# Starting the first projection on the latent tokens alone, with the first weight chunk loaded in two halves

## The reference, cut to what matters

```python
silu_c, silu_cc = jax.nn.silu(c), jax.nn.silu(c_ctx)
# layer 0
shift, scale, gate       = jnp.split(silu_c  @ w_ada[0] + b_ada[0], 3, axis=-1)
shift_c, scale_c, gate_c = jnp.split(silu_cc @ w_ada[0] + b_ada[0], 3, axis=-1)
u  = x   * (1.0 + scale)   + shift        # 256 x 1024, the latents
uc = ctx * (1.0 + scale_c) + shift_c      # 256 x 1024, the other tokens
p  = u @ a_w_in[0]                        # 1024 x 2560: q, k, v and a gate
pc = uc @ a_w_in[0]
```

## Time and profile before

| what | us |
|---|---|
| median of three executions | 1200.04 (1199.06 to 1200.21) |
| the profiled execution | 1197.66 |
| its span, first to last instruction | 1195.8 |
| TensorE busy, of the span | 1145.7 (96%) |
| VectorE busy, of the span | 540.7 (45%) |
| DMA, mean over the span | 261 GB/s |

### The profile page before, as it was taken

How to read it: one execution, slowest core, us unless ns; L and a number is a source line. 1 busy time by engine, 2 the same in 40 slices (tenths; PEclk the granted TensorE clock), 3 DMA queues, 4 the chain that set the end, 5 groups by cost and what they waited for, 6 DMA issues and landing times.

```text
span 1195.8 us, 17528 instructions
## 1 busy us (share of the span) xinstructions
PE 1145.7 (96%) x7148; PEld 735.3 (61%) x7148; DVE 540.7 (45%) x1236; ACT 297.2 (25%) x722; POOL 22.8 (2%) x33
## 2 busy tenths in 40 slices
PE   4999999989999999999999899999999999999997
PEld 3486876668878888668886684444444444444442
DVE  3353439987566430792699722222222222222223
ACT  0000128860240001570521622211111111111112
POOL 0000000000000001120000000000000000000000
PEclk9999999999999999999999998999999999999999
DMA  9852219014343225467375987999999999999991
GB/s 339 330 211 71 71 70 353 2 39 171 119 166 119 93 71 167 112 181 235 141 287 192 349 205 313 427 428 427 428 429 429 427 429 426 430 429 429 429 420 64
DMA packets 82334, 312.59 MB, mean 261 GB/s; under 512 B 18129, under 2 KB 19228, under 8 KB 69338
## 3 DMA queue, kind: packets, MB, share of 16 engines
q1 hardware_dynamic: 78528, 309.03, 66.8%
q10 hardware_dynamic: 3530, 2.44, 0.7%
q0 software_dynamic: 208, 0.17, 0.1%
HBM read 310.45 MB, written 1.18 MB: 261 GB/s over the span
## 4 chain that ended last, share of the span: by engine, by line
PE 83%; DVE 12%; DMA 2%; ACT 2%; issue 1%; SPq 1%; DVEq 0%; ACTq 0%
PE ps L1270 18%; PE ps L903 17%; PE ps L1303 9%; PE ps L1236 5%; PE ps L1006 5%; PE ps L1248 5%; DVE G L2180 4%; PE ps L968 2%; PE ps L941 2%; PE ps L852 2%; PE ps L1111 2%; PE ps L1087 2%; PE ps L954 2%; PE ps L755 2%; DMA ring<-in_a_w_in 2%; DVE soft L1859 1%
## 5 line engine op out<-in xcount | busy, mean ns | idle before, releaser
L1270 PE MATMUL ps<-ring,prob 128*64 128x512 f32 x704 | 188.1, 592 | 0.0
L1270 PEld LDWEIGHTS ps<-ring,prob 128*64 128x64 f32 x704 | 60.9, 137 | 100.0 <-issue 99.9
L2335 DVE TENSOR_TENSOR prob<-ps,prob 128x512 f32<-128x512 f32 x16 | 17.2, 1076 | 191.9 <-PE ps L1270 191.9
L1303 PE MATMUL ps<-ring,prob 128*64 128x512 f32 x352 | 78.0, 595 | 0.0
L903 PE MATMUL ps<-U,ring 128*128 128x256 f32 x304 | 69.9, 380 | 1.6 <-DVE Q L2025 1.3
L1270 PE MATMUL ps<-K,prob 128*64 128x512 f32 x160 | 70.3, 592 | 0.0
L1236 PEld LDWEIGHTS ps<-bias,U 128*128 128x128 f32 x512 | 60.0, 196 | 13.7 <-issue 13.7
L1414 ACT ACTIVATE prob<-ps,soft 128x512 f32<-128x512 f32 (+2 forms) x112 | 65.0, 591 | 10.5 <-DVE soft L1864 8.5
L2343 DVE TENSOR_TENSOR probT<-ps,cst 128x512 f32<-128x512 f32 x32 | 22.1, 692 | 94.6 <-PE ps L1303 94.6
L903 PEld LDWEIGHTS ps<-U,ring 128*128 128x128 f32 x304 | 57.4, 190 | 10.1 <-DVE Q L2025 1.7
L1236 PE MATMUL ps<-bias,U 128*128 128x128 f32 x512 | 63.1, 283 | 0.0
(11 more groups left out here) (377 smaller groups left out, 1824.8 us busy)
## 6 DMA issues: line engine op xcount, KB each, us to landing
ring<-in_w_exp_gate SPq DMA_DIRECT2D x22, 2048.0 KB, 18.1
ring<-in_w_exp_up SPq DMA_DIRECT2D x20, 2048.0 KB, 16.5
ring<-in_w_exp_down SPq DMA_DIRECT2D x20, 2048.0 KB, 19.2
ring<-in_w_ada SPq DMA_DIRECT2D x12, 2048.0 KB, 16.4
ring<-in_w_mod SPq DMA_DIRECT2D x12, 2048.0 KB, 10.3
ring<-in_b_w_in SPq DMA_DIRECT2D x8, 2048.0 KB, 9.0
ring<-in_a_w_in SPq DMA_DIRECT2D x5, 2048.0 KB, 17.6
ring<-in_w_in SPq DMA_DIRECT2D x5, 2048.0 KB, 10.4
```

Of the source, the lines that this page charges most:

```text
L1270: last = mm(ps[x * CAP:(x + 1) * CAP, 2 + i, :], xg[:, k, x * CAP:(x + 1) * CAP], chunk(n, 2 * i + x, turn)[0][:, k, :], start=(k == 0), s ...
L1303: last = mm(ps[x * CAP:(x + 1) * CAP, 5 + c, :], hidT[:, k, x * CAP:(x + 1) * CAP], chunk(n, 4 + x, turn)[0][:, k, c * 512:(c + 1) * 512], ...
```

## The change

SP issues chunk 1 ahead of the latents' rows. Chunk 2, the first `a_w_in` chunk, is loaded in two DMAs of 1024 KB: its lower four row tiles in its old place in the order, with a semaphore of their own (`lower_in`), its upper four behind chunk 4. The context rows go behind the lower half.

TensorE streams chunks 0 and 1 first, then turns the latents' first four feature tiles, does both folds, turns the other four (two tiles to a bank) and the taps. Each lower job is now two jobs of 256 tokens: four matmuls on the latents, and later four on the context, into the two halves of the same bank. The turns of the context rows stand between the latents' jobs. The upper jobs are as before, over all 512 tokens, behind all lower ones. VectorE's copies of rows and its modulation follow that order: the first four latent tiles one by one, all further ones two at a time (128 x 512), and latents and context modulated apart in the lower features. The load of `a_sink` shares the semaphore of the taps.

The diff, cut to its core:

```diff
                 w = IN[src][l, :, c * COLS:(c + 1) * COLS].rearrange("(k p) n -> p k n", p=P)
-                sp.dma_start(slot(n), w).then_inc(full[n % SLOTS], 16)
-                if n in (0, 1):
-                    rows = IN[("x", "ctx")[n]][0].rearrange("(t p) f -> p t f", p=P)
-                    sp.dma_start(xrows[:, 2 * n:2 * n + 2, :], rows).then_inc(x_in[n], 16)
+                if n == PLACE["a_in"][0]:
+                    first_w = w
+                    sp.dma_start(slot(n)[:, 0:4, :], w[:, 0:4, :]).then_inc(lower_in, 16)
+                else:
+                    sp.dma_start(slot(n), w).then_inc(full[n % SLOTS], 16)
+                if n in (1, 2):
+                    rows = IN[("x", "ctx")[n - 1]][0].rearrange("(t p) f -> p t f", p=P)
+                    sp.dma_start(xrows[:, 2 * n - 2:2 * n, :], rows).then_inc(x_in[n - 1], 16)
+                if n == 4:
+                    first = PLACE["a_in"][0]
+                    sp.dma_start(slot(first)[:, 4:KT, :], first_w[:, 4:KT, :]).then_inc(full[first % SLOTS], 16)
...
             def turn_taps():
-                pe.wait_ge(taps_in, 16)
-                pe.wait_ge(vec_ok, 1)
+                pe.wait_ge(taps_in, 32)
+                pe.wait_ge(x_ok, 4)
...
-            def turn_rows(half):
-                pe.wait_ge(x_in[half], 16)
-                for j in range(KT):
-                    i = half * KT + j
-                    if i >= 4:
-                        pe.wait_ge(x_ok, i - 3)
+            def turn_rows(half, js, bank):
+                for i, j in enumerate(js):
                     for t in range(2):
-                        last = tr(ps[:, 1 + j % 4, t * P:(t + 1) * P], xrows[:, 2 * half + t, j * P:(j + 1) * P], ident)
-                    last.then_inc(pe_x, 1)
+                        last = tr(ps[:, bank, i * S + t * P:i * S + (t + 1) * P],
+                                  xrows[:, 2 * half + t, j * P:(j + 1) * P], ident)
+                last.then_inc(pe_x, 1)
...
             stream("ada0", 0, 5)
-            turn_rows(0)
             stream("ada0", 1, 6)
+            pe.wait_ge(x_in[0], 16)
+            for j in range(4):
+                turn_rows(0, (j,), 1 + j)
             fold("ada0", 0, 0, 2, 7)
-            turn_rows(1)
+            fold("ada0", 1, 0, 2, 7)
+            turn_rows(0, (4, 5), 5)
+            turn_rows(0, (6, 7), 6)
             turn_taps()
-            fold("ada0", 1, 0, 2, 7)
...
+            def lower_job(i, c0):
+                for k in range(4):
                     if i == 0:
-                        pe.wait_ge(u_ok, k + 1)
+                        pe.wait_ge(u_ok, (k + 1 if c0 == 0 else 4 + k + 1))
+                    mm(ps[:, i, c0:c0 + S], slot(PLACE["a_in"][0])[:, k, i * P:(i + 1) * P], uT[:, k, c0:c0 + S],
+                       start=(k == 0 and c0 == 0), stop=False)
...
+            pe.wait_ge(lower_in, 16)
+            lower_job(0, 0)
+            lower_job(1, 0)
+            pe.wait_ge(x_in[1], 16)
+            turn_rows(1, (0, 1), 7)
             pe.wait_ge(taps_ok, 1)
+            turn_rows(1, (2, 3), 4)
+            lower_job(2, 0)
+            lower_job(3, 0)
+            pe.wait_ge(x_ok, 7)
+            turn_rows(1, (4, 5), 7)
+            pe.wait_ge(x_ok, 8)
+            turn_rows(1, (6, 7), 4)
+            lower_job(0, S)
+            stream("ada0", 2, 5)
+            lower_job(1, S)
+            stream("ada0", 3, 6)
+            lower_job(2, S)
+            pe.wait_ge(x_ok, 10)
+            fold("ada0", 2, 0, 2, 4)
+            fold("ada0", 3, 0, 2, 4)
+            lower_job(3, S)
             landed(PLACE["a_in"][0])
-            half_job(0, range(4))
-            half_job(1, range(4))
-            stream("ada0", 2, 5)
-            half_job(2, range(4))
-            stream("ada0", 3, 6)
-            fold("ada0", 2, 0, 2, 4)
-            half_job(3, range(4))
-            fold("ada0", 3, 0, 2, 4)
             for i in range(4):
-                half_job(i, range(4, KT))
+                upper_job(i)
                 beside(i)
...
             dve.wait_ge(vec_ok, 1)
             step(take_half(0, 7))
-            dve.wait_ge(x_ok, 2 * KT)
+            dve.wait_ge(x_ok, 4)
             settle()
-            modulate(0, range(4))
+            for j in range(4):
+                v.tensor_scalar(uT[:, j, 0:S], H[:, j, 0:S], mod[:, 0, 8 + j, 0:1], mod[:, 0, j, 0:1],
+                                ALU.mult, ALU.add).then_inc(u_ok, 1)
+            take_rows(0, 4, 5, 5)
+            take_rows(0, 6, 6, 6)
+            dve.wait_ge(pe_vec, 2)
+            v.tensor_copy(conv_taps[:, :, :],
+                          ps[:, 4, 256:384].rearrange("p (c k) -> p c k", c=4)[:, :, 0:CONV_W]).then_inc(taps_ok, 1)
+            take_rows(1, 0, 7, 7)
+            take_rows(1, 2, 4, 8)
+            dve.wait_ge(x_ok, 8)
+            for j in range(4):
+                v.tensor_scalar(uT[:, j, S:T], H[:, j, S:T], mod[:, 0, 8 + j, 1:2], mod[:, 0, j, 1:2],
+                                ALU.mult, ALU.add).then_inc(u_ok, 1)
+            take_rows(1, 4, 7, 9)
+            take_rows(1, 6, 4, 10)
             take_half(1, 4).then_inc(mod_ok, 1)
             dve.wait_ge(mod_ok, 1)
+            dve.wait_ge(x_ok, 10)
             modulate(0, range(4, KT))
```

More of the change, by code:

```diff
@@ L383, in build @@
         table_in = sem("table_in")
-        cst_in, vec_in, sink_in = sem("cst_in"), sem("vec_in"), sem("sink_in")
+        cst_in, vec_in = sem("cst_in"), sem("vec_in")
         x_in, taps_in, taps_ok = [sem("x_in"), sem("ctx_in")], sem("taps_in"), sem("taps_ok")
@@ L389, in build @@
         pe_x, x_ok = sem("pe_x"), sem("x_ok")
+        lower_in = sem("lower_in")
         sil_ok = sem("sil_ok")
@@ L721, in turn_taps @@
             def turn_taps():
-                pe.wait_ge(taps_in, 16)
-                pe.wait_ge(vec_ok, 1)
+                pe.wait_ge(taps_in, 32)
+                pe.wait_ge(x_ok, 4)
                 for c in range(4):
-                    last = tr(ps[:, 0, 256 + 32 * c:256 + 32 * c + CONV_W], crows[:, c * P:(c + 1) * P],
+                    last = tr(ps[:, 4, 256 + 32 * c:256 + 32 * c + CONV_W], crows[:, c * P:(c + 1) * P],
                               ident[0:CONV_W, 0:CONV_W])
                 last.then_inc(pe_vec, 1)
-            def turn_rows(half):
-                pe.wait_ge(x_in[half], 16)
-                for j in range(KT):
-                    i = half * KT + j
-                    if i >= 4:
-                        pe.wait_ge(x_ok, i - 3)
+            def turn_rows(half, js, bank):
+                for i, j in enumerate(js):
                     for t in range(2):
-                        last = tr(ps[:, 1 + j % 4, t * P:(t + 1) * P], xrows[:, 2 * half + t, j * P:(j + 1) * P], ident)
-                    last.then_inc(pe_x, 1)
+                        last = tr(ps[:, bank, i * S + t * P:i * S + (t + 1) * P],
+                                  xrows[:, 2 * half + t, j * P:(j + 1) * P], ident)
+                last.then_inc(pe_x, 1)
             def stream(stage, c, bank):
@@ L815, in src_ready @@
                 if stage == "a_in":
-                    return u_ok, k + 1
+                    return u_ok, 4 + k + 1
                 return nm["rms1", "out"], k + 1
@@ L844, in rotate @@
                 mm(ps[:, 4 + n % 2, 0:S], rotm, src, start=True, stop=True).then_inc(rot_done, 1)
-            def half_job(i, ks):
-                for k in ks:
+            def lower_job(i, c0):
+                for k in range(4):
                     if i == 0:
-                        pe.wait_ge(u_ok, k + 1)
-                    last = mm(ps[:, i, :], slot(PLACE["a_in"][0])[:, k, i * P:(i + 1) * P], uT[:, k, :],
-                              start=(k == 0), stop=(k == KT - 1))
-                if k == KT - 1:
-                    last.then_inc(st["a_in"], 1)
@@ new lines, in upper_job @@
+            def upper_job(i):
+                for k in range(4, KT):
+                    if i == 0:
+                        pe.wait_ge(u_ok, 4 + k + 1)
+                    last = mm(ps[:, i, :], slot(PLACE["a_in"][0])[:, k, i * P:(i + 1) * P], uT[:, k, :],
+                              start=False, stop=(k == KT - 1))
+                last.then_inc(st["a_in"], 1)
+            pe.wait_ge(lower_in, 16)
+            lower_job(0, 0)
+            lower_job(1, 0)
+            pe.wait_ge(x_in[1], 16)
@@ L1353, in _ @@
             act.dma_start(crows, IN["conv_w_2"][0]).then_inc(taps_in, 16)
-            act.dma_start(sink[:, :], IN["a_sink"].broadcast_to([P, NH])).then_inc(sink_in, 16)
+            act.dma_start(sink[:, :], IN["a_sink"].broadcast_to([P, NH])).then_inc(taps_in, 16)
             act.wait_ge(cst_in, 16)
@@ L1648, in _, with take_rows @@
             v.tensor_copy(vec[:, :], ps[:, 0, 0:NVEC]).then_inc(vec_ok, 1)
[L1649 to L1655, removed]
+            for j in range(4):
+                dve.wait_ge(pe_x, j + 1)
+                v.tensor_copy(H[:, j, 0:S], ps[:, 1 + j, 0:S]).then_inc(x_ok, 1)
```

(10 more changed lines are left out.)

## The result

The changed kernel took 1192.37 us (median of 4, 1190.63 to 1195.35) against 1199.62 for the kernel before (median of 4, 1199.06 to 1200.21): ratio 0.9932, 95% interval 0.9910 to 0.9955. Its profiled execution took 1195.35 (span 1193.6), the slowest of the four and only 2.3 less than that of the kernel before: the profile shows less than the times do, and why is most of what follows.

What follows compares the result with a forecast made beforehand. The start was taken as bound by bytes in a DMA queue. A 4.9 us earlier start plus 1.3 of bubble saved, less 2.3 of context transposes moved, gave 3.8: 1200.04 - 3.8 = 1196.2 us, range 1194.7 to 1199.2.

Steps and rivals of the forecast that it cites:

- 8 transposes at 2.32/16 = 0.145: TensorE's start, before the first lower job: each group of eight transposes takes 1.16 us.
- `x`: Load of the latents' rows at the start: takes the place chunk 1 ended on and lands at 21.1 us.
- VectorE did not hide wholly: Start: first latent tile ready at 23.9, next each 0.32 later against 0.45 per matmul, so VectorE hides.
- 256-column jobs cost nothing more: Lower jobs: 64 records of 256 columns take 14.3 us, against 14.27 before; halved width costs nothing within 0.2.
- the bubble of 1.3: TensorE's gap between last fold and upper jobs, 1.3 us, is covered by the last lower job and gone.
- no resource with a clock of its own: After 60 us: none is left, later loads move with the engines, so nothing takes the gain back.
- Rivals 1 to 3: 1: loads wanted first land later, gain halved, 0.12; 2: gain taken back later, 1200.0, 0.05; 3: transfers end together, 1201.0, 0.07.
- Rival 4: Start: waits for chunk 1 or `x` bring TensorE's slow pace to the turns; gain 1, 1199; chance 0.03.
- carried over: Whole kernel: the median shown is 2.4 us above the profiled execution; the 3.8 gain applied to it gives 1196.2.
- Does it reach the end?: Prediction's section on everything after the upper jobs: all 3.8 us reach the end, profiled execution 1193.9, median 1196.2.
- after 2.36 us of idleness line 852 ran at full pace at once: First lower job of the kernel before: the observation given against a slow TensorE pace after waits.
- All 3.8 pass through: From the upper jobs to the end: the whole gain of 3.8 us stays.

Runs made afterwards that it cites:

- the repeat: The kernel before, profiled and timed once more with no edit: 1199.99 us, ratio 0.9998.
- the work alone: The changed kernel with loads in the old order and the first `a_in` chunk in one piece, against the kernel before: 1199.35 us, ratio 0.9984.
- the kernel before with the fill at the start: The kernel before plus ten unread 128-column products in the idle stretch ahead of the first lower job: 1198.41 us, ratio 0.9994.
- the one with late fills: The kernel before plus unread 384-column products in two later idle stretches, four near 341 us and two near 720: 1193.44 us, ratio 0.9952.
- the gap of 2.4 us: The changed kernel plus a TensorE wait for the context rows ahead of its first lower job: 1198.03 us, ratio 0.9988 to the kernel before.
- The changed kernel with the two late fills: The changed kernel plus unread 384-column products, four near 336 us and two near 716: 1188.47 us (0.9916 of the kernel before), again 1189.48 (0.9914).

## Why the prediction was wrong

**The balance.** The timed executions of the experiments together: the kernel before 1200.2 (78, mean clock 0.9909), the changed one 1192.8 (14, 0.9926): 7.4, give or take 1.2. At the slope that the kernels show among their own executions, some 1060 us for each 1.0 of clock (1040 to 1110, by which kernels are taken), 1.8 of it go with the clock. At equal clock the difference is 5.6, give or take 0.6; the traces show a fixed shift of 5.1 from the start. The 5.1 alone would have given 1194.9, inside the range.

**Terms of the fixed part: 5.1 against 3.8.** *Transposes.* The step "8 transposes at 2.32/16 = 0.145" was mis-sized. The row held a pace of VectorE: `turn_rows` waited for one copy of 0.34 us per pair of transposes once its four banks were full. With waits gone and two tiles to a bank they run at 0.87/8 = 0.11. That saves 0.2 to 0.4 of the start and 2.32 - 1.74 = 0.6 of the work behind it. *`x`* landed at 20.7, not 21.1. VectorE did not hide wholly: the job waited 0.18 for its first tile. Together the start was 23.61 and not 24.15, the work to the upper jobs 20.25 and not 20.85. The last 0.1 lies in the first upper jobs (7.03 against 7.13).

**What was right.** The order and the landings of the loads; that 256-column jobs cost nothing more; that the bubble of 1.3 goes; that `ctx`, chunks 3 and 4 and the upper half are in time; that no resource with a clock of its own takes the gain back: the shift of 5.1 at 170 us is still 5.1 when the load of `b_w_out` is issued (469.64 against 464.50). Rivals 1 to 3 did not happen. The form "needs both parts" was not predicted but follows from it.

**The step that failed**, besides the two sizes above, is a term put at nothing: the lower clock behind the idle stretch of 2.4 us of the kernel before, which the change removes. Rival 4 set it aside, and "carried over" in *Does it reach the end?* rests on that. I judged from one execution: "after 2.36 us of idleness line 852 ran at full pace at once". That execution was the lucky one. The idle stretch is followed by the lower clock in four of six profiles, 1.5 us on average over the six, and the change takes it away; I had considered the lower clock only as something that the change could bring. The sign that was there: the median shown was 2.4 us above the profiled execution. I treated this as a constant to be added to both kernels. It may well have been in part the price of the stretch that the change removes.
The Trainium skill (TensorE: Matmul & The Clock Gate, HAM oscillation) warns that long gaps in which TensorE waits for a DMA make its clock fall. I did not weigh that rule for the kernel before. By its figure it speaks of longer gaps than this one; the trace of the repeat has a granted clock of 0.51 behind 2.37 us, and there the measurement decides.

**A second term that the prediction put at nothing** lies between 470 and 545 us. "All 3.8 pass through" takes the rest of the program as unchanged. But in all five profiles of the kernel before TensorE stands still for 0.65 to 1.27 us inside the stream at line 755, after 121 of its 128 records, and the profile shows nothing that it waits for:

```profile
490.08 0.42 PE L755 MATMUL ps<-ring,sil 128*32 128x128 f32 x7 [0.65 <-issue]
```

From the issue of the load of `b_w_out` to that of `w_in` these five take 73.5 to 75.1 us. The three profiles of the changed kernel don't show the stop, and take 72.5 or 72.6. That is the growth of the shift from 5.1 to 6.5 in the result, 1.5 us on average. It doesn't come from the earlier start: the work alone, the kernel before with the fill at the start and the one with late fills have 72.5 too. What the stop is, and whether the timed executions have it as often, is not shown.

**What stays open.** The 5.1 fixed and the 1.5 at the start make 6.6 of 7.4; with the 1.5 of the stop they would make 8.1. Both sums are within the 1.2 of uncertainty, and the 5.6 at equal clock lies between 5.1 and 6.6, so the times don't settle how much of the excess over 5.1 is clock and how much is the stop. That filling the stretch brings 1.5 us is not shown by times (0.8 in one pair, the other sign in another); what is shown is that with the gap of 2.4 us the lower clock is there in six of eight profiles, and in none of the eight without it (six with the changed start, two with the stretch filled). Why the lower clock in the third attention comes in some executions and not in others stays open too.

**A version that beats both.** The changed kernel with the two late fills: 4.1 us under the changed kernel by means on one chip, 0.9914 of the kernel before.

## What to carry to other kernels

A mean duration of a row can hold another engine's pace: look at whether the instruction waits inside its group before using it for a new order. A profile is one execution: where the timed ones lie elsewhere, read their mean clock, and ask for each idle stretch of TensorE whether it is followed by the lower clock in other executions, since a change that removes the stretch can be paid twice, once for its length and once for the clock. And look at what a change shifts far behind its own place: compare landmarks to the end of the program. Compare kernels at equal clock when a few us matter.

## What the runs showed of the hardware

An idle stretch of 2.4 us on TensorE, 12 us after its first dense work, was followed by the lower level, 1.2 GHz, in four of six profiles of the kernel before. With two unread products of 384 columns in the 1.4 us of idleness ahead of the router the clock was 1.00 over it in five of five profiles, without them in one of thirteen. Together with four more near 334 us they were worth 4 us in the changed kernel (means, one chip), and 6 in the kernel before, nearly as much as the rebuilt start; in the profile of the latter the stop near 490 us is gone too, so not all of its 6 need be clock.
